# The xLSTM stage of a hybrid decoder block: output copied out of PSUM, norm in batches of two chunks, two buffers for a step's operands

## What is computed

```
s    = (q_c . k_c) * w_intra
num  = w_inter * (q_c . C_prev) + s . v_c
den  = w_inter * (q_c . n_prev) + sum(s)
h    = num / max(|den|, exp(-m))
C_next = decay * C_prev + sum(w_state * k_c (x) v_c)      # n_next likewise
...
mu, var = mean(h), mean((h - mu)^2)            # over the 128 channels of a head
out  = (h - mu) * rsqrt(var + LN_EPS) * norm_g * sigmoid(o_pre)
```

## Time and profile before

| | us |
|---|---|
| median of 3 runs | 2379.95 (2377.66 to 2383.66) |
| the profiled execution: its own time | 2376.8 |
| its span, first to last instruction | 2375.0 |
| the mLSTM loop in it (VectorE's first k_state to its last gated) | 318.00 to 410.94 |

### The profile page before, as it was taken

How to read it: one execution, slowest core, us unless ns; L and a number is a source line. 1 busy time by engine, 2 the same in 40 slices (tenths; PEclk the granted TensorE clock), 3 DMA queues, 4 the chain that set the end, 5 groups by cost and what they waited for, 6 DMA issues and landing times. The chain is left out here.

```text
span 2375.0 us, 32365 instructions
## 1 busy us (share of the span) xinstructions
PE 2162.7 (91%) x10370; PEld 1790.0 (75%) x10371; DVE 1706.0 (72%) x2002; ACT 1208.5 (51%) x1225; POOL 540.5 (23%) x541
## 2 busy tenths in 40 slices
PE   5999855789679999999999999999999999999993
PEld 4787855668458887887888878887887888878772
DVE  4688765745785665778779886787976798677774
ACT  3422132233164554557557664766764576565753
POOL 1001111101521111214224221322411242121401
PEclk9999967999689999999999999999999999999997
DMA  6123270641296666779879886897986798687964
GB/s 174 54 80 133 79 126 14 197 165 45 106 367 223 214 223 194 255 274 310 304 228 373 313 282 227 298 327 256 360 316 206 229 369 312 228 270 258 316 223 180
DMA packets 285815, 540.84 MB, mean 228 GB/s; under 512 B 37155, under 2 KB 53587, under 8 KB 284659
## 3 DMA queue, kind: packets, MB, share of 16 engines
q1 hardware_dynamic: 260306, 490.51, 59.9%
q0 software_dynamic: 25440, 49.47, 8.0%
HBM read 513.06 MB, written 64.57 MB: 243 GB/s over the span
## 5 line engine op out<-in xcount | busy, mean ns | idle before, releaser
L2322 DVE TENSOR_TENSOR ex_w_lo<-ex_raw,ex_w_hi 128x2048 fp32r<-128x2048 f32 x408 | 928.7, 2288 | 265.2 <-ACT ex_w_hi L2216 197.5
L2216 ACT CAST ex_w_hi<-ex_raw 128x2048 fp32r<-128x2048 f32 x371 | 708.3, 1912 | 255.6 <-PE ex_ps_l L2536 80.8
L2127 POOL TENSOR_TENSOR ex_passed<-ex_ident 128x1 f32<-128x1 f32 x136 | 107.9, 793 | 1215.7 <-ACT ex_y L2258 1196.4
L2535 PE MATMUL ex_ps_g<-ex_w_hi,ex_x_hi 128*128 128x512 f32 x784 | 309.1, 394 | 16.3 <-issue 6.4
L2535 PE MATMUL ex_ps_l<-ex_w_hi,ex_x_hi 128*128 128x512 f32 x784 | 308.8, 394 | 1.5 <-DVE ex_w_lo L2322 1.5
L2536 PE MATMUL ex_ps_g<-ex_w_lo,ex_x_hi 128*128 128x512 f32 x784 | 306.5, 391 | 0.0
L2536 PE MATMUL ex_ps_l<-ex_w_lo,ex_x_hi 128*128 128x512 f32 x784 | 305.2, 389 | 0.0
L2535 PE MATMUL ex_ps_y<-ex_w_hi,ex_h_hi 128*128 128x512 f32 x544 | 217.4, 400 | 6.8 <-DVE ex_h_lo L2358 6.8
L2539 PE MATMUL ex_ps_g<-ex_w_hi,ex_x_lo 128*128 128x512 f32 x544 | 212.7, 391 | 0.0
L2539 PE MATMUL ex_ps_l<-ex_w_hi,ex_x_lo 128*128 128x512 f32 x544 | 212.0, 390 | 0.0
L2536 PE MATMUL ex_ps_y<-ex_w_lo,ex_h_hi 128*128 128x512 f32 x544 | 212.0, 390 | 0.0
(11 more groups left out here) (458 smaller groups left out, 3764.0 us busy)
## 6 DMA issues: line engine op xcount, KB each, us to landing
ex_raw<-in_w_up_dram SPq DMA_DIRECT2D x272, 1024.0 KB, 8.0
ex_raw<-in_w_down_dram SPq DMA_DIRECT2D x136, 1024.0 KB, 8.2
st_tab<-tabs SPq DMA_DIRECT2D x8, 1408.0 KB, 7.2
pr_raw<-in_w_in_dram SPq DMA_DIRECT2D x10, 1024.0 KB, 5.6
tabs<-pr_x POOLq DMA_DIRECT2D x32, 256.0 KB, 2.3
por_raw<-in_w_out_dram SPq DMA_DIRECT2D x16, 256.0 KB, 5.6
t<-mix_sig_o SPq DMA_DIRECT2D x8, 512.0 KB, 2.6
fi_h<-h SPq DMA_DIRECT2D x8, 512.0 KB, 7.8
```

What stands on the lines that cost most here:

```text
L2127: pool.tensor_tensor(passed[:, :], ident[:, 0:1], ident[:, 0:1], ALU.add).then_inc(passed_done, 1)
L2216: nc.scalar.copy(w_hi[:, j % SPLIT, :, :], raw[:, j % RAW, :, :]).then_inc(hi_done, 1)
L2322: v.tensor_tensor(w_lo[:, j % SPLIT, :, :], raw[:, j % RAW, :, :], w_hi[:, j % SPLIT, :, :].bitcast(F32), ALU.subtract).then_inc(lo_done, 1)
L2535: pe.matmul(to[:, :], hi_in[:, b, kk, :], w_hi[:, s, k, :], start=first, stop=False)
```

## The change

A chunk's output is copied from PSUM to SBUF by ScalarE (`copy_out`, two copies of 128 x 258), and statistics, denominator and norm read the copy. The norm's scalars are made for two chunks at once (`variance`, `power`, `scales`; the last two chunks singly), at the end of steps 2, 4, 6 and 7 and after the loop. The scaling (`norm`) of chunk c-2 stands in ScalarE's step c, transposition and gate of chunk c-3 in step c of TensorE and VectorE. q_inter, intra, k_state and normed get two buffers each, so that their waits are for a step earlier. On TensorE the state product comes ahead of spread_m, and scores(c+1) ahead of the output. The state update of C now waits for the output of the step before (`out_ready`, c), the output waits for the copy of the step before (`out_copied`), and the k_state of the last chunk, which nothing reads, is left out. Four setup arrays share the memory of the copy. The core of the diff:

```diff
-        f_abs = sb("f_abs", [HEADS, T], F32)
-        log_f = sb("log_f", [HEADS, T], F32)
-        not_first = sb("not_first", [HEADS, T], F32)
-        carry = sb("carry", [HEADS, T], F32)
+        out = sb("out", [P, NC, HEADS, HD + 1], F32)
+        early = out[:, :, :, :].rearrange("p c h e -> p (c h e)")
+        f_abs = early[0:HEADS, 0 * T:1 * T]
+        log_f = early[0:HEADS, 1 * T:2 * T]
+        not_first = early[0:HEADS, 2 * T:3 * T]
+        carry = early[0:HEADS, 3 * T:4 * T]
...
-        q_inter = sb("q_inter", [P, HEADS, CH], F32)
-        intra = sb("intra", [P, HEADS, CH], F32)
-        k_state = sb("k_state", [P, HEADS, HD], F32)
+        q_inter = sb("q_inter", [P, 2, HEADS, CH], F32)
+        intra = sb("intra", [P, 2, HEADS, CH], F32)
+        k_state = sb("k_state", [P, 2, HEADS, HD], F32)
         C = sb("C", [P, 2, HEADS, HD + 1], F32)
-        normed = sb("normed", [P, HEADS, HD], F32)
...
+        normed = sb("normed", [P, 2, HEADS, HD], F32)
+        denom = sb("denom", [P, NC, HEADS], F32)
+        inv = sb("inv", [P, NC, HEADS], F32)
+        stats = sb("stats", [P, NC, HEADS, 6], F32)
+        mean_var = sb("mean_var", [P, NC, HEADS, 2], F32)
+        var_h = sb("var_h", [P, NC, HEADS], F32)
+        rstd = sb("rstd", [P, NC, HEADS], F32)
+        scale, shift = rstd, denom
...
+        BATCHES = [slice(0, 2), slice(2, 4), slice(4, 6), slice(6, 7), slice(7, 8)]
+        NORM_AT = [batch.stop for batch in BATCHES]
+        LAG = 3
...
+                def power(i):
+                    batch = BATCHES[i]
+                    pool.wait_ge(var_done, i + 1)
+                    pool.tensor_tensor(rstd[:, batch, :], var_h[:, batch, :], neg_half[:, 0:batch.stop - batch.start, :], ALU.pow).then_inc(pow_done, 1)
                 for c in range(NC):
                     pool.wait_ge(inter_done, c + 1)
-                    if c:
-                        pool.wait_ge(out_ready, c)
-                    pool.tensor_tensor(q_inter[:, :, :], q[:, :, steps(c)], w_inter[:, :, :], ALU.mult).then_inc(q_done, 1)
-                    pool.wait_ge(var_done, c + 1)
-                    pool.tensor_tensor(rstd[:, :], var_h[:, :], neg_half[:, :], ALU.pow).then_inc(pow_done, 1)
+                    if c >= 2:
+                        pool.wait_ge(out_ready, c - 1)
+                    pool.tensor_tensor(q_inter[:, c % 2, :, :], q[:, :, steps(c)], w_inter[:, :, :], ALU.mult).then_inc(q_done, 1)
+                    if c in NORM_AT:
+                        power(NORM_AT.index(c))
+                power(len(BATCHES) - 1)
...
+                def copy_out(c):
+                    act.wait_ge(out_ready, c + 1)
+                    for i in range(2):
+                        ins = nc.scalar.copy(out[:, c, 2 * i:2 * i + 2, :],
+                                             ps_o[i][:, 0:2 * (HD + 1)].rearrange("p (h e) -> p h e", h=2))
+                    ins.then_inc(out_copied, 1)
+                def norm(c):
+                    act.wait_ge(shift_done, 1 + [i for i, batch in enumerate(BATCHES) if batch.start <= c < batch.stop][0])
+                    if c >= 2:
+                        act.wait_ge(t_ready, c - 1)
+                    for h in range(HEADS):
+                        ins = nc.scalar.activation(normed[:, c % 2, h, :], out[:, c, h, 0:HD], ACT.Identity,
+                                                   scale=scale[:, c, h:h + 1], bias=shift[:, c, h:h + 1])
+                    ins.then_inc(normed_done, 1)
                 weights(0)
                 for c in range(NC):
                     if c + 1 < NC:
                         weights(c + 1)
-                    act.wait_ge(shift_done, c + 1)
-                    if c:
-                        act.wait_ge(t_ready, c)
...
-                                                   scale=scale[:, h:h + 1], bias=shift[:, h:h + 1])
-                    ins.then_inc(normed_done, 1)
+                    copy_out(c)
+                    if c >= LAG - 1:
+                        norm(c - (LAG - 1))
+                for c in range(NC - LAG + 1, NC):
+                    norm(c)
...
+                def state(c):
+                    pe.wait_ge(k_done, c + 1)
+                    if c:
+                        pe.wait_ge(c_done, c)
+                    for h in range(HEADS):
+                        to = ps_c[h // 2][:, (h % 2) * (HD + 1):(h % 2 + 1) * (HD + 1)]
+                        mm = pe.matmul(to, k_state[:, c % 2, h, :], v_aug[:, c, h, :], start=True, stop=True)
+                    mm.then_inc(c_ready, 1)
+                def output(c):
+                    pe.wait_ge(intra_done, c + 1)
+                    if c:
+                        pe.wait_ge(q_done, c + 1)
+                        pe.wait_ge(c_done, c)
+                        pe.wait_ge(out_copied, c)
+                    for h in range(HEADS):
+                        mm = pe.matmul(o_bank(h), intra[:, c % 2, h, :], v_aug[:, c, h, :], start=True, stop=(c == 0))
+                        if c:
+                            mm = pe.matmul(o_bank(h), q_inter[:, c % 2, h, :], C[:, c % 2, h, :], start=False, stop=True)
+                    mm.then_inc(out_ready, 1)
                 spread_m(0)
                 turn_k(0)
                 scores(0)
                 for c in range(NC):
                     if c + 1 < NC:
+                        state(c)
                         spread_m(c + 1)
...
                         turn_k(c + 1)
-                    if c:
-                        turn_normed(c - 1)
...
-                    if c + 1 < NC:
                         scores(c + 1)
-                turn_normed(NC - 1)
+                    if c >= LAG:
+                        turn_normed(c - LAG)
+                    output(c)
+                for c in range(NC - LAG, NC):
+                    turn_normed(c)
...
+                def statistics(c):
+                    v.wait_ge(out_copied, c + 1)
+                    for h in range(HEADS):
+                        ins = v.bn_stats(stats[:, c, h, :], out[:, c, h, 0:HD])
+                    link(ins)
+                def variance(batch):
+                    den = out[:, batch, :, HD]
+                    link(v.scalar_tensor_tensor(denom[:, batch, :], den, -1.0, exp_neg_m[:, batch, :], ALU.mult, ALU.max))
+                    link(v.tensor_tensor(denom[:, batch, :], den, denom[:, batch, :], ALU.max))
+                    v.reciprocal(inv[:, batch, :], denom[:, batch, :])
+                    for c in range(batch.start, batch.stop):
+                        for h in range(HEADS):
+                            ins = v.bn_aggr(mean_var[:, c, h, :], stats[:, c, h, :])
+                    link(ins)
+                    link(v.tensor_tensor(var_h[:, batch, :], mean_var[:, batch, :, 1], inv[:, batch, :], ALU.mult))
+                    link(v.tensor_tensor(var_h[:, batch, :], var_h[:, batch, :], inv[:, batch, :], ALU.mult))
+                    v.tensor_scalar(var_h[:, batch, :], var_h[:, batch, :], LN_EPS, None, ALU.add).then_inc(var_done, 1)
+                def scales(i):
+                    batch = BATCHES[i]
+                    v.wait_ge(pow_done, i + 1)
+                    link(v.tensor_tensor(scale[:, batch, :], rstd[:, batch, :], inv[:, batch, :], ALU.mult))
+                    v.scalar_tensor_tensor(shift[:, batch, :], mean_var[:, batch, :, 0], -1.0, scale[:, batch, :],
+                                           ALU.mult, ALU.mult).then_inc(shift_done, 1)
                 mask_m(0)
                 v.wait_ge(cols_set, 5)
                 v.wait_ge(small_in, 16)
                 for c in range(NC):
-                    v.wait_ge(k_ready, c + 1)
-                    if c:
-                        v.wait_ge(c_ready, c)
-                    v.tensor_tensor(k_state[:, :, :], by_head(ps_k),
-                                    w_state[:, c, :].unsqueeze(2).to_broadcast([P, HEADS, HD]), ALU.mult).then_inc(k_done, 1)
+                    if c + 1 < NC:
+                        v.wait_ge(k_ready, c + 1)
+                        if c >= 2:
+                            v.wait_ge(c_ready, c - 1)
+                        v.tensor_tensor(k_state[:, c % 2, :, :], by_head(ps_k),
+                                        w_state[:, c, :].unsqueeze(2).to_broadcast([P, HEADS, HD]), ALU.mult).then_inc(k_done, 1)
                     v.wait_ge(s_ready, c + 1)
                     v.wait_ge(weight_done, c + 1)
-                    if c:
-                        v.wait_ge(out_ready, c)
-                    v.tensor_tensor(intra[:, :, :], by_head(ps_s), weight[:, :, :], ALU.mult).then_inc(intra_done, 1)
+                    if c >= 2:
+                        v.wait_ge(out_ready, c - 1)
+                    v.tensor_tensor(intra[:, c % 2, :, :], by_head(ps_s), weight[:, :, :], ALU.mult).then_inc(intra_done, 1)
                     if c + 1 < NC:
                         mask_m(c + 1)
+                    if c:
+                        statistics(c - 1)
```

(91 more changed lines are left out.)

15 lines of the change are left out of this document (3 added, 12 removed).

## The result

| | before | changed |
|---|---|---|
| median of 6 runs, us | 2380.36 (2377.66 to 2383.66) | 2365.76 (2359.41 to 2370.82) |
| ratio, 95% interval | | 0.9927 (0.9912 to 0.9942) |
| profiled execution: time, span, us | 2376.8, 2375.0 | 2366.74, 2364.9 |
| mLSTM loop, first k_state to last gate, us | 92.9 | 77.2 |

The change makes the kernel 14.6 us faster, 0.73%. The forecast was 20.4 us; the loop itself became 15.8 us shorter in the profiled execution.

The account below looks back on a forecast made before the run. A chain through engines, not a full engine, bounds the loop; taking the norm off it saves 24.1 us, less 3.7 for the low clock, so 20.4 less: 2356.4 profiled, 2359.6 as median, range 2350 to 2370.

Parts of the forecast that it names:

- forecast case: Whole kernel: 16 to 24 us less than before, 2356 to 2364 us; chance 0.60.
- the clock stays low in most steps: Rival: TensorE low for four to six loop steps and the tail; only 13 to 17 us less, 2363 to 2367; chance 0.17.
- the four signs of being wrong: mask_m's wait much over 2 us; ScalarE's weights late behind a norm; VectorE awaiting transpositions before a gate; loop clock below 0.78.
- The chain on VectorE as the new bound: Loop: VectorE's own chain sets the step, 6.8 us without a batch and 10.0 with one, at the high clock.
- The added wait: Loop: with the state product ahead of spread_m, VectorE idles about 1.6 us a step before mask_m.
- The power of eight elements: GpSimd in batch steps: taken as 1.01 us, no growth with size; twice that would add 3 us over three steps.
- The low clock: TensorE after batch steps: state product and spread_m cost 1.83 us more; two falls taken, 3.7 us, bounds 0 and 11.
- The tail: From step 7 to the last gate: statistics, variance, gates, scales, last norm and transposition; 377.1 after step 7, end at 386.8.
- The held scale: VectorE in steps 2, 4 and 6: scale starts with GpSimd's q_inter and costs 1.13 us again, 1.33 with shift.
- Nothing gives the gain back: After the loop: the next stage starts at its barrier with s5's loads long landed, so the loop's gain stays.
- the one in which norm(c-2) delays ScalarE's weights: Rival: late norm holds up weights(c+2), so the norm stays on the path; 4 to 8 us less, 2372 to 2376; chance 0.06.
- The slower one: Rival: TensorE at the low clock throughout becomes the bound, 11.7 us a step; 8.5 us slower, 2388.5; chance 0.02.

Follow-up runs that it names:

- spread_m_first: Changed kernel with spread_m(c+1) ahead of the state product again, as in the kernel before; 2360.7 us, ratio 0.9888 to the kernel before.
- gated_first: Changed kernel with gated(c-3) ahead of scale and shift on VectorE; 2368.7 us, ratio 0.9927 to the kernel before.
- after_again: The changed kernel run once more, unaltered, as the measure for the others; 2365.2 us, ratio 0.9933 to the kernel before.
- changed_beside: The changed kernel, unaltered, run on one chip beside a kernel with further edits; 2370.5 us, ratio 0.9928 to the kernel before.
- the kernel with three edits: Changed kernel with spread_m before state product, gate before scale and shift, last scales between gated(5) and gated(6); run twice, ratios 0.9875 and 0.9870.

## Why the prediction was right, and where it was off

The time, 2365.8, lies inside 2350 to 2370, and the sign and the main mechanism were right: buffers alone give nothing, the copy alone costs 9 us, and the gain comes once the norm is late. The gain was 14.6 where 20.4 stood. By its size it lies outside the forecast case (2356 to 2364) and in the rival "the clock stays low in most steps" (2363 to 2367); by its cause it doesn't belong there, since only steps 3, 5 and the tail (0.50 throughout) were low. Of the four signs of being wrong that the prediction names, three came in the first profile: mask_m's wait well over 2 us in two steps, VectorE waiting for transpositions before a gate, and a loop clock of 0.74. They point at the same thing: the low clock cost more than the sum had for it. Distances of k_state, forecast (with 1.83 in steps 3 and 5) and measured in the first profile:

| | step 0 | 1 | 2 | 3 | 4 | 5 | 6 | from step 7 on |
|---|---|---|---|---|---|---|---|---|
| forecast | 5.3 | 5.7 | 8.8 | 8.6 | 10.0 | 8.6 | 10.0 | 15.4 |
| measured | 5.4 | 5.6 | 9.3 | 9.5 | 10.5 | 9.5 | 10.7 | 16.6 |

The forecast sums to 72.5, the measurement to 77.2. Of the 4.7 between them, 1.7 lie in the three batch steps, 1.8 in steps 3 and 5, 1.2 in the tail.

- **The chain on VectorE as the new bound** held, and so did its items: mask_m starts 3.02 us after k_state(2) (2.94), statistics from SBUF take 0.86 (0.89 from PSUM), and steps 0 and 1 are right to 0.2 us. The full step without a batch at the high clock, 6.8, was never seen: steps 3 and 5 had a low clock, at least in part, in all three profiles of this kernel.
- **The added wait** was forecast at 1.6 us a step and was 1.63 and 1.74 in steps 1 and 2, at the high clock. The forecast counted it as a given part of the new order; spread_m_first shows that the order cost 6 to 8 us of the loop (77.2 and 75.4 against 69.0).
- **The power of eight elements** is the mis-sized term of the batch steps: taken as 1.01 from rows of one and four elements, it took 1.64 to 1.67. The other end of its bound, 2.0, was nearer. Scale waited 0.7 for it in each of steps 2, 4 and 6; 0.2 of that was made good by the variance, laid out at 1.84 and measured at 1.66. The prediction read "no growth with size" from the one group of one element that took 1.04. The kernel before has two more, and they say otherwise:

```profile
L1600 POOL TENSOR_TENSOR por_rstd<-por_meansq,por_neg_half 128x1 f32<-128x1 f32 x8 | 4.5, 560 | 72.9 <-DVE por_meansq L1794 72.9
L328 POOL TENSOR_TENSOR pr_rstd<-pr_meansq,pr_neg_half 128x1 f32<-128x1 f32 x8 | 4.4, 552 | 33.5 <-DVE pr_meansq L542 33.5
```

  An estimate from 0.55 for one element and 1.01 for four gives 0.15 more for each element and 1.6 for eight. Why the third group took 1.04 isn't known.
- **The low clock** fell on steps 3 and 5 as forecast, but its price was too small. State product and spread_m cost the 1.83; the transposition ahead of the gate cost 0.98 more, since at the low level it no longer ends under the C update, and the work left over met k_state(4) and k_state(6), where mask_m waited 1.97 and 2.18 instead of 1.6. So a fall costs some 3.0 to 3.3 us, not 1.83: 2.7 in its own step (9.5 against 6.8) and 0.4 or 0.6 in the next.
- **The tail** was 1.2 longer: the last output ran at the low clock, statistics(7) waited 0.61 for its copy, gated(5) waited 0.37 for its transposition, and that of chunk 6 stood 1.27 us between two gates instead of 0.8.
- **The held scale** came as laid out, 1.13 to 1.15 in three steps. The two denominator operations with both inputs in SBUF were never beside q_inter, and took 0.17 each. By that rule (the Trainium skill, SBUF — State Buffer, Who interferes with whom) they could have been held; no run here had them beside a GpSimd instruction. In gated_first scale started 0.33 us behind q_inter, ended with it and took 0.87, which agrees with the rule.
- **"Nothing gives the gain back"** was too sure for a single profile: s5 took 89 to 92 us in the three profiles of the changed kernel, 87 before. In the medians it doesn't show.
- Of the rivals, the one in which norm(c-2) delays ScalarE's weights didn't happen: norm(0) ended at 340.2, mask_m(4) at 344.0. The slower one needed the low clock throughout; the loop's mean was 0.74 in the first profile, against 0.78 before. The reordering of scores ahead of the output, also part of the change, was not run by itself.

## What to carry to other kernels

Where an in-order engine holds work that nothing in the recurrence needs, moving it late frees the path, but more buffers alone do nothing as long as the queue's order stays. Lay out the new step engine by engine, and look at each exchange of two groups that comes with the change: here the exchange of spread_m and the state product cost about half of what the late norm gained. Where rows of one operation disagree, as those of the power did, don't take the one that says that size costs nothing. Price an operation for the size that it will have, and let a fall of the clock count for every group of the step that has slack at the high level only.

## What the runs showed of the hardware

- GpSimd's power -0.5 took 1.01 us for 128 x 4 and 1.64 to 1.67 for 128 x 8; for 128 x 1 two groups took 0.55 and 0.56, a third 1.04.
- A VectorE product of 128 x 4 or 128 x 8 from two SBUF tiles takes 0.16 us alone (128 x 4), 1.13 to 1.15 where it started 0.05 to 0.07 behind a GpSimd product of 128 x 512, and 0.86 or 0.87 where it started 0.33 behind.
- ScalarE's copy of 128 x 258 from PSUM takes 0.38 us, two of them 0.65; four activations of 128 x 128 with a scale and a bias per partition 1.65 from SBUF and 1.50 from PSUM.
- The granted clock fell at different places in three profiled executions of one kernel (step 3: 9.5, 8.2 and 9.5 us), and once it fell in the middle of a group after idles of only 1.1 us. A state product behind an idle of 3.8 us ran at the high level in two profiles (after_again, gated_first) and at the low level in two (the first and changed_beside). The loop of one kernel varies by 1.7 us, and that of the kernel with three edits by 3.
